# Query copies of the stick-breaking heads made in the projection stage, and a single identity matrix

## What is computed

```python
def stick_breaking_attention(q, k, v):
    # q, k, v (B, T, H, dh), H = 8 heads of dh = 64
    z = jnp.einsum('bqhd,bkhd->bhqk', qb, k).astype(jnp.float32) * scale
    causal = kpos[None, :] < tq[:, None]
    log_beta = jax.nn.log_sigmoid(z)
    log_keep = jnp.where(causal, log_beta - z, 0.0)
    later = lax.cumsum(log_keep, axis=3, reverse=True) - log_keep
    a = jnp.where(causal, jnp.exp(log_beta + later), 0.0)
    return jnp.einsum('bhqk,bkhd->bqhd', a, v)
...
h = rmsnorm(x, norm_attn[layer])
proj = h @ w_in[layer]
o_nsa = nsa_attention(...)          # compressed, selected and window branches
o_sb = stick_breaking_attention(qkv[:, :, 0], qkv[:, :, 1], qkv[:, :, 2])
mixed = merge[:, :, 0] * (o_nsa @ w_up_nsa) + merge[:, :, 1] * (o_sb @ w_up_sb)
x = x + mixed @ w_out
x = x + square(relu(rmsnorm(x, norm_mlp) @ w_ff1)) @ w_ff2
```

## Time and profile before

| | us |
|---|---|
| median of 3 runs | 808.18 |
| their range | 807.93 to 808.45 |
| the profiled execution's own time | 807.72 |
| its span, from the first to the last instruction | 805.9 |
| PE busy in that span | 785.0 |
| ACT busy | 329.2 |
| DVE busy | 390.5 |
| POOL busy | 362.8 |

### The profile page before, as it was taken

How to read it: one execution, slowest core, us unless ns; L and a number is a source line. 1 busy time by engine, 2 the same in 40 slices (tenths; PEclk the granted TensorE clock), 3 DMA queues, 4 the chain that set the end, 5 groups by cost and what they waited for, 6 DMA issues and landing times.

```text
span 805.9 us, 11632 instructions
## 1 busy us (share of the span) xinstructions
PE 785.0 (97%) x3984; PEld 642.5 (80%) x3984; DVE 390.5 (48%) x780; ACT 329.2 (41%) x583; POOL 362.8 (45%) x468
## 2 busy tenths in 40 slices
PE   5999999999999999999999999999999999999995
PEld 4878988878877677678888888888888888888895
DVE  6555446775646565645544286541155114521234
ACT  6333324488766566566244333322223212321221
POOL 4354343611112222226546486665476556655530
PEclk9999999999999999999999999999999999999998
DMA  8842133210240101025322332332232233223213
GB/s 267 314 129 101 53 108 102 79 52 28 45 138 27 53 27 53 27 79 183 104 99 85 105 94 89 104 105 81 102 104 87 96 104 97 85 104 104 84 48 105
DMA packets 25477, 77.60 MB, mean 96 GB/s; under 512 B 3710, under 2 KB 6966, under 8 KB 25183
## 3 DMA queue, kind: packets, MB, share of 16 engines
q1 hardware_dynamic: 23932, 75.25, 28.1%
q10 hardware_dynamic: 1507, 1.84, 0.8%
HBM read 73.90 MB, written 2.13 MB: 94 GB/s over the span
## 4 chain that ended last, share of the span: by engine, by line
PE 89%; DVE 4%; ACT 3%; issue 1%; DMA 1%; POOL 1%; SPq 0%; DVEq 0%
PE bank L1169 65%; PE bank L1443 2%; PE bank L1425 2%; PE bank L1362 2%; PE bank L1476 2%; PE bank L1481 2%; PE bank L1480 2%; PE bank L1404 1%; PE bank L1405 1%; DMA wraw<-in_panels 1%; PE bank L1374 1%; PE bank L1187 1%; PE bank L1188 1%; PE bank L1189 1%; PE bank L1269 1%
## 5 line engine op out<-in xcount | busy, mean ns | idle before, releaser
L489 POOL TENSOR_TENSOR wlo<-wraw,whi 128x256 fp32r<-128x256 f32 x460 | 355.3, 804 | 407.9 <-ACT whi L528 211.4
L546 ACT ACTIVATE whi<-wraw 128x1024 fp32r<-128x1024 f32 x48 | 50.9, 1061 | 154.7 <-PE bank L1169 152.4
L1169 PE MATMUL bank<-hh,wlo 128*128 128x512 f32 x304 | 83.0, 397 | 0.5 <-DVE gm L995 0.3
L1169 PE MATMUL bank<-hl,whi 128*128 128x512 f32 x304 | 82.4, 393 | 0.0
L1169 PE MATMUL bank<-hh,whi 128*128 128x512 f32 x304 | 81.4, 392 | 0.0
L528 ACT ACTIVATE whi<-wraw 128x1024 fp32r<-128x1024 f32 x57 | 59.9, 1053 | 47.1 <-DMA wraw<-in_panels 28.0
L1107 DVE TENSOR_TENSOR x_res<-bank,x_res 128x512 f32 (+1 forms) x28 | 19.4, 693 | 117.4 <-PE bank L1169 117.4
L1169 PE MATMUL bank<-h2h,wlo 128*128 128x512 f32 x256 | 66.0, 391 | 0.0
L1169 PE MATMUL bank<-h2h,whi 128*128 128x512 f32 x256 | 65.5, 389 | 0.0
L1169 PE MATMUL bank<-h2l,whi 128*128 128x512 f32 x256 | 65.5, 389 | 0.0
L1169 PEld LDWEIGHTS bank<-hh,whi 128*128 128x128 f32 x304 | 56.2, 188 | 10.9
(11 more groups left out here) (240 smaller groups left out, 1249.3 us busy)
## 6 DMA issues: line engine op xcount, KB each, us to landing
wraw<-in_panels SPq DMA_DIRECT2D x117, 512.0 KB, 3.3
w1k<-in_w SPq DMA_DIRECT2D x1, 2048.0 KB, 9.5
w1v<-in_w SPq DMA_DIRECT2D x1, 2048.0 KB, 15.0
hank<-bias_by_distance SPq DMA_DIRECT2D x4, 512.0 KB, 6.5
x_res<-in_xT SPq DMA_DIRECT2D x4, 512.0 KB, 4.3
out_dram<-x_res SPq DMA_DIRECT2D x16, 128.0 KB, 1.9
xs<-in_xT SPq DMA_DIRECT2D x4, 256.0 KB, 7.4
xs<-in_xT ACTq DMA_DIRECT2D x4, 256.0 KB, 6.9
```

The source lines that it names most:

```text
L489: ins = nc.gpsimd.tensor_tensor(wlo[:, s, k:k + 2], wraw[s][:, k:k + 2], whi[:, s, k:k + 2].bitcast(F32), ALU.subtract)
L546: A(whi[:, s], wraw[s][:], ACT.Copy).then_inc(w_hi, 1)
L1169: ins = M(b[:, cols], lhs, (xl if a == 1 else xh)[:, row + k, cols], start=(m == 0), stop=(m == 23))
```

## The change

All four sets of copies are made among the projections: `queries_twice(p - 1)` behind the rounding of the keys' panel of pair p, and that of pair 3 behind the last panel's `split`. There are four buffers `sq_odd` in place of two, two of them in memory that is unused in that stage. The copies in heads 0, 2 and 4 are gone. `ident_r` is the only identity; it is loaded as fp32 into a passing buffer `ident_in`, cast by DVE ahead of its first bias copy, and PE's transposes read it as fp32.

```diff
-        ident = place("ident", [P, P])
...
         ident_r = place("ident_r", [P, P], F32R)
+        ident = ident_r[:].bitcast(F32)
...
-        sq_odd = [place("sq_odd0", [P, T], F32R), None]
+        sq_odd = [place(f"sq_odd{p}", [P, T], F32R, at=at) for p, at in enumerate((None, tmp_at, tmp_at + 2048, None))]
...
+        ident_in = place("ident_in", [P, P], at=at_sbv + 6400)
...
-        sq_odd[1] = place("sq_odd1", [P, T], F32R, at=tmp_at)
...
-            sp.dma_start(ident[:], cst[:, 2 * P + 2 * T:3 * P + 2 * T]).then_inc(table_in, 16)
+            sp.dma_start(ident_in[:], cst[:, 2 * P + 2 * T:3 * P + 2 * T]).then_inc(table_in, 16)
...
             def queries_twice(p):
 
+                stored(act, ("pan", P_SQK + 2 * p))
                 for o in range(2):
-                    A(sq_odd[p % 2][GROUP[o]], sq_h[GROUP[1], p], ACT.Copy).then_inc(q_twice, 1)
+                    A(sq_odd[p][GROUP[o]], sq_h[GROUP[1], p], ACT.Copy).then_inc(q_twice, 1)
                 act.wait_ge(q_twice, 3 * p + 2)
                 A(sq_h[GROUP[1], p], sq_h[GROUP[0], p], ACT.Copy).then_inc(q_twice, 1)
...
-                if i == 3:
-                    stored(act, ("pan", P_SQK))
-                    queries_twice(0)
+                if qk and p:
+                    queries_twice(p - 1)
                 if i in (1, 3):
                     cmp_exp(2 + i // 2)
                 split(P_SQK + i + RING)
+            queries_twice(PAIRS - 1)
...
-                if h % 2 == 0 and h // 2 + 1 < PAIRS:
-                    stored(act, ("pan", P_SQK + 7))
-                    queries_twice(h // 2 + 1)
...
+            dve.wait_ge(table_in, 16 * 3)
+            V.tensor_copy(ident_r[:], ident_in[:]).then_inc(cast_done, 1)
             bias_half(0)
...
-            dve.wait_ge(table_in, 16 * 3)
+            dve.wait_ge(cast_done, 1)
             dve.wait_ge(cst_in, 16 * 2)
             V.tensor_copy(negtri[:], cstb[:, 0:P]).then_inc(cast_done, 1)
-            V.tensor_scalar(negones[:], ident[:], 0.0, -1.0, ALU.mult, ALU.add).then_inc(cast_done, 1)
+            V.tensor_scalar(negones[:], ident, 0.0, -1.0, ALU.mult, ALU.add).then_inc(cast_done, 1)
             V.tensor_copy(diag_r[:], cstb[:, P:2 * P]).then_inc(cast_done, 1)
-            V.tensor_copy(ident_r[:], ident[:]).then_inc(cast_done, 1)
...
             b = claim(pe_, "rcol")
             pe_.wait_ge(rst, 1)
+            pe_.wait_ge(cast_done, 1)
...
-                queries = sq_odd[p % 2][:] if odd else sq_h[:, p]
+                queries = sq_odd[p][:] if odd else sq_h[:, p]
```

More of the change, by code:

```diff
@@ L1251, in _ @@
             pe_.wait_ge(rst, 1)
+            pe_.wait_ge(cast_done, 1)
             for r in range(RT):
-                ins = nc.tensor.transpose(b[:, P * r:P * r + P], rstd_b[:, P * r:P * r + P], ident[:])
+                ins = nc.tensor.transpose(b[:, P * r:P * r + P], rstd_b[:, P * r:P * r + P], ident)
             filled(ins, "rcol")
@@ L1275, in _ @@
             for m in range(2):
-                ins = nc.tensor.transpose(b[:, P * m:P * m + P], hid[:, P * m:P * m + P], ident[:])
+                ins = nc.tensor.transpose(b[:, P * m:P * m + P], hid[:, P * m:P * m + P], ident)
             filled(ins, "hidT")
@@ L1305, in cmp_transpose @@
                 for g in range(G):
-                    ins = nc.tensor.transpose(b[:, P * g:P * g + P], c_g[:, r % 2, HG * g:HG * g + HG, :].rearrange("p j c -> p (j c)"), ident[:])
+                    ins = nc.tensor.transpose(b[:, P * g:P * g + P], c_g[:, r % 2, HG * g:HG * g + HG, :].rearrange("p j c -> p (j c)"), ident)
                 if r >= 2:
-                    ins = nc.tensor.transpose(b[0:2 * NB, 2 * P:3 * P], c_k[:].rearrange("p g n -> p (g n)"), ident[:])
+                    ins = nc.tensor.transpose(b[0:2 * NB, 2 * P:3 * P], c_k[:].rearrange("p g n -> p (g n)"), ident)
                 filled(ins, ("ct", r))
@@ L1424, in turn @@
                 for k in range(r + 1):
-                    ins = nc.tensor.transpose(b[:, P * k:P * k + P], ns[u % 4][:, P * k:P * k + P], ident[:])
+                    ins = nc.tensor.transpose(b[:, P * k:P * k + P], ns[u % 4][:, P * k:P * k + P], ident)
                 filled(ins, ("t", u))
```

## The result

The changed kernel takes 812.5 us in the median (810.72 to 813.83, 6 runs), against 808.05 us before (807.38 to 808.45, 6 runs): a ratio of 1.0055, 95% interval 1.0042 to 1.0069, so 4.4 us slower. The forecast was 810.4 us, with a range up to 811.7. The profiled execution took 811.58 us, and its span 809.7 against 805.9, 3.8 us more.

A forecast was written before the change was run, and what follows sets the result against it. PE was taken to bound the kernel, except heads 0 and 1, bound by the ACT and DVE chain. Copies ahead of head 0 (+2.79) less head 0's removed slot (-0.60), all else 0, gave +2.19 us: 808.18 to 810.4, range 809.2 to 811.7.

The forecast's parts named there:

- Where the work is bound: Stick heads: heads 0 and 1 bound by the ACT and DVE chain, heads 2 to 6 by PE.
- The removed copies: Three slots of 1.98 us leave heads 0, 2, 4; only head 0's counts, giving back 0.60 us.
- the sum: All terms: 0 identity, 0 pair 1, +2.79 pairs 2 and 3, -0.60 head 0, 0 heads 2 and 4: +2.19 us.
- The copies of pair 1: Behind panel 5, 1.98 us hidden in ACT's idle 6.77 us; claimed to cost 0.
- The added copies of pairs 2 and 3: Two slots of 1.98 us ahead of head 0, less 1.17 us idle: exps and sums of head 0 2.79 us later.
- The rival with overlapping copies: Six copies ahead of head 0 at a pitch of 0.49 us: +1.2 us, 809.4 us; chance 0.09.
- The identity: DVE's 0.215 us cast moved before its first bias copy, where DVE idles 2.50 us: zero, give or take 0.2 us.
- The clock: Rival: clock falls on PE's new 2.8 us idle time before sums of head 0: +3.4 us, 811.6 us; chance 0.07.
- The direct part: Delay from copies ahead of head 0, less head 0's removed slot, at full clock: 2.19 us.
- The range: 809.2 us (overlapping copies with a spread of 0.2) to 811.7 us (above the clock and second-place rivals).

The follow-up runs named there:

- the idle time filled: Changed kernel plus twelve unread 512-column matmuls on PE between the gate products and sums of head 0: 810.54 us, ratio 1.0028 against the kernel before.
- the longer series: The changed kernel again, nothing altered, timed in more rounds with each run's granted clock: 811.34 us in the median, ratio 1.0048 against the kernel before.
- one slot ahead: Changed kernel with pair 3's copies made in head 2, so only pair 2's stand ahead of head 0: 808.65 us, ratio 1.0021.
- eight copies ahead: Spread copies (none ahead of or in head 0) plus eight extra ACT copies of 64 by 512 ahead of head 0: 813.55 us, ratio 1.0059.

## Why the prediction was too low

**Where the work is bound: right for PE.** PE's only new idle time is at sums(0), ended by L1022 (L1021 after the change), and heads 2 to 6 take nothing back. Its idle time before sums(7) is 1.37 us, as before.

**The removed copies: right in kind, a little high in size.** The slots of heads 2 and 4 brought nothing. That of head 0 gave back 0.43 us (8.49 to 8.06 in the table), where the sum had 0.60: `stick_weights` ended 5.27 us behind DVE's minimum with the idle time filled, and 5.11 had been taken from head 2.

**The copies of pair 1: a term put at nothing.** The sum has 0 for them, because they stand in ACT's idle time. They cost 0.33 us all the same, through POOL and DVE: the addition of 0.50 us in place of 0.17. The prediction followed the late `split` to POOL and PE, and not to DVE.

**The added copies of pairs 2 and 3: right.** From the rounding of the last panel to the exps of head 0 it is 161.82 - 155.57 = 6.25 us in the changed kernel, against 158.37 - 154.92 = 3.45 us before, 2.80 us more; the sum said 2.79. The rival with overlapping copies is out: a slot took 1.98 us here too (156.79 to 158.77). So the rule of the Trainium skill that it rested on (ScalarE: Activation LUTs, section What ACT_TABLE_LOAD costs, an overlap of about 93 ns) does not hold for these half-height copies, while the full-height one at 152.72 us is followed 0.49 us later.

**The identity: right**, 808.05 us alone.

**The clock: the step that failed.** The forecast had nothing in its sum for a slower clock behind PE's new idle time. The prediction had it as a rival, at its place and with a price (+3.4 us, 811.6), and gave it 0.07. Two arguments were wrong. It took the clock's 1.00 through the waits of the stick heads as evidence, but those waits lasted 0.9 us and the new one 2.9; and it took the fall at 800 us, behind all work, as if that much idle time were needed. In all three profiles of the changed kernel the clock is at half there, for 3.4 or 6.8 us. That adds 0.9 us in the short form and 2.0 us in the long one, which the prediction did not have. That its +3.4 us comes near the short form is in part luck: it has 1.2 us for the clock in place of 0.9, and lacks the 0.33 us of pair 1.

**The direct part: 2.6 us, 2.19 forecast.** With the idle time filled it is 0.33 us for pair 1, 2.73 at sums(0) counted from the last panel (166.53 - 154.94 against 163.78 - 154.92), less the 0.43 given back. This alone would be 810.6 to 810.7 us, inside the range. The spans of the three profiled runs of the changed kernel are accounted for: up to sums(0) they are 2.93, 2.80 and 3.37 us late, in which -0.13, -0.26 and 0.33 us are the different starts at panel 5, and the rest, about 3.05 us each, is 0.33 for pair 1 and 2.72 for the copies. The longer interval behind it adds 8.93 - 8.49, 10.10 - 8.49 and 8.96 - 8.49, which gives 3.4, 4.4 and 3.8 us for spans of 809.3, 810.3 and 809.7.

**The range** ended at 811.7 us, between the short and the long form. The likeliest case should have been 2.6 us plus a fall of one form or the other, which by these numbers is about 811.5 or 812.6 us.

What stays open: which form a run gets, and why two of the fifteen runs of the changed kernel in the result and the longer series, at 810.17 and 810.72 us with a mean clock of 0.997, seem to have none, which fits the 810.6 us of the direct part. No profile caught such a run. Nor does anything here explain what the three slowest runs of the result (813.33 to 813.83 us) have above 812.6, the run of 817.99 us, or those of 811.85 and 814.66 us with one slot ahead. The median of 812.5 us in the result lies above the 811.34 of the later session, and the share of the two forms would account for it; this is argued, not shown.

## What to carry to other kernels

Work taken off ACT where PE does not wait for it (heads 2 and 4) was worth nothing here, and put ahead of the stage's first link it cost its whole length less the idle time that stood there. Compare the places by the wait that ends last, not by how busy the engine is. A place where the engine itself idles is not free for certain either: follow what it releases later, on every engine, as POOL's late `low` cost DVE 0.33 us here. Take the different starts of two executions off before comparing their timelines. And a new idle time of PE can have a second price, the slower clock behind it, as those of 2.0 to 4.3 us had here: look for it in short stretches of the granted clock, and fill the idle time, if with nothing else then with matmuls that nobody reads, or place the work elsewhere.

## What the runs showed of the hardware

The granted clock has two levels in all these traces, 1.00 and 0.50, that is 2.4 and 1.2 GHz, which is also what the Trainium skill says (TensorE: Matmul & The Clock Gate, section Part 1: The HAM clock gate). A value such as 0.54 or 0.80 is a stretch that has both. What I had not expected is how little it takes: idle times of 0.82, 1.38 (before sums(7)) and 1.65 us left the clock alone in the profiled runs, one of 2.02 us brought it down, and it came down either during the idle time (with eight copies ahead at 168.5 us, sums(0) started at 169.41) or up to 1.0 us after PE had resumed (in the result at 168.2 us, with the sums started at 167.15). Twelve matmuls whose result is thrown away made the kernel 0.8 us faster. No kernel here puts one between 1.65 and 2.02 us there.

The mean clock of a run, to three digits, can hide such a fall: 0.996 was read with one and without. And at the start of a run the column itself does not show the slow clock that the earlier trace rows show by the lengths of the matmuls. Of the kernel before:

```profile
10.00:12.00 2.00, 2.00 (x6) 1.61 (x6) 2.00 (x4) 1.98 (x4) 0.00 (x0) 1.00 1.02 393
```

So the lengths of single matmuls, as 0.41 in place of 0.28 us at 168.20, are the check on the column.
